# The joins between mixer, dense layer and routing: weight splits moved behind block 1's norm, a first product in halves, the router as one 16-column operand, a gather in four banks

## The reference, cut to what matters

```
for l in range(2):
    h = rms_norm(x, norm_mix[l])
    x = x + hybrid_mixer(h, w_in[l], conv_w[l], ..., w_out[l])     # conv, group norm, silu; gated unit
    h = rms_norm(x, norm_ffn[l])
    if l % 2 == 0:
        x = x + swiglu(h, ffn_wg[0], ffn_wu[0], ffn_wd[0])         # 1024 -> 2816 -> 1024
    else:
        logits = h @ router                                        # 1024 -> 8
        top_vals, top_idx = top_k(logits, 2); gates = softmax(top_vals)
        x = x + sum over e of gate[:, e] * swiglu(h, wg[e], wu[e], wd[e])
x = rms_norm(x, norm_final)
# then second_block: meta tokens, two attentions, gates, output product, norm
```

## Time and profile before

| | |
|---|---|
| median of 3 runs | 1587.92 us (1583.66 to 1600.85) |
| profiled execution, its own time | 1595.88 us |
| its span on the core | 1594.1 us |
| TensorE busy | 1521.7 us (95%) |
| VectorE busy | 1112.6 us (70%) |
| ScalarE busy | 902.7 us (57%) |
| mean granted TensorE clock | 0.966 of full speed |
| mean HBM traffic over the span | 263 GB/s |

### The profile page before, as it was taken

One profiled execution on the slowest core, in us unless ns is written; L12 is line 12 of the kernel. 1 busy time (PEld: TensorE's weight loads), 2 busy tenths in 40 slices (PEclk: granted clock), 3 DMA queues, 4 the chain that ended last, 5 costly groups with the idle time before them and its releaser, 6 DMA issues.

```text
span 1594.1 us, 19419 instructions
## 1 busy us (share of the span) xinstructions
PE 1521.7 (95%) x7672; PEld 1283.5 (81%) x7672; DVE 1112.6 (70%) x974; ACT 902.7 (57%) x765; POOL 98.6 (6%) x110
## 2 busy tenths in 40 slices
PE   6989999979889999999999999999999599999997
PEld 6869998878688888888888888888888496777785
DVE  6975555359668888888888888888788543333555
ACT  4554344235537677776777767676776353343452
POOL 3600000035010000000000000000100100000000
PEclk9999999989979999999999999999999797998999
DMA  9457974443429999999999999999998442232250
GB/s 303 146 168 238 323 250 172 132 138 129 146 76 404 357 379 378 364 391 355 386 366 366 394 348 404 350 387 370 368 400 308 149 159 79 80 104 81 80 185 27
DMA packets 118955, 408.21 MB, mean 256 GB/s; under 512 B 5840, under 2 KB 31616, under 8 KB 118896
## 3 DMA queue, kind: packets, MB, share of 16 engines
q1 hardware_dynamic: 114576, 392.84, 67.4%
q0 software_dynamic: 3104, 10.22, 1.8%
q10 hardware_dynamic: 1216, 4.33, 0.7%
HBM read 400.02 MB, written 19.40 MB: 263 GB/s over the span
## 4 chain that ended last, share of the span: by engine, by line
PE 86%; DVE 8%; ACT 2%; DMA 2%; issue 2%; ACTq 0%; SPq 0%; POOL 0%; DVEq 0%; POOLq 0%
PE ps L460 24%; PE ps L461 23%; PE ps L462 23%; DVE yT L1826 3%; DVE low L444 1%; PE ps L456 1%; PE ps L2433 1%; PE ps L2157 1%; PE ps L2121 1%; PE ps L2159 1%; PE ps L2158 1%; ACT high L433 1%; DMA raw<-in_moe_wu 1%; PE ps L1214 1%; PE ps L1235 1%
## 5 line engine op out<-in xcount | busy, mean ns | idle before, releaser
L450 DVE TENSOR_TENSOR low<-raw,high 128x2816 fp32r<-128x2816 f32 (+1 forms) x168 | 516.2, 3090 | 100.9 <-ACT high L439 100.8
L439 ACT ACTIVATE high<-raw 128x2816 fp32r<-128x2816 f32 (+1 forms) x168 | 428.4, 2560 | 104.3 <-PE ps L462 60.5
L460 PE MATMUL ps<-high,xTm_hi 128*128 128x512 f32 (+2 forms) x1152 | 428.0, 372 | 13.0 <-DVE xTm_lo L1863 6.2
L461 PE MATMUL ps<-low,xTm_hi 128*128 128x512 f32 (+2 forms) x1152 | 422.7, 367 | 0.0
L462 PE MATMUL ps<-high,xTm_lo 128*128 128x512 f32 (+2 forms) x1152 | 422.4, 367 | 0.0
L444 DVE TENSOR_TENSOR low<-raw,high 128x2816 fp32r<-128x2816 f32 (+2 forms) x72 | 203.1, 2827 | 81.0 <-ACT high L433 81.0
L460 PEld LDWEIGHTS ps<-high,xTm_hi 128*128 128x128 f32 x1152 | 217.8, 189 | 48.1 <-DVE xTm_lo L1863 6.7
L462 PEld LDWEIGHTS ps<-high,xTm_lo 128*128 128x128 f32 x1152 | 217.8, 189 | 28.4
L461 PEld LDWEIGHTS ps<-low,xTm_hi 128*128 128x128 f32 x1152 | 217.9, 189 | 28.0
L433 ACT ACTIVATE high<-raw 128x2816 fp32r<-128x2816 f32 (+2 forms) x72 | 168.4, 2343 | 113.4 <-PE ps L462 93.2
L460 PE MATMUL ps<-high,eT_hi 128*128 128x512 f32 x352 | 142.1, 404 | 0.0
(11 more groups left out here) (361 smaller groups left out, 1795.6 us busy)
## 6 DMA issues: line engine op xcount, KB each, us to landing
raw<-in_moe_wg SPq DMA_DIRECT2D x64, 1408.0 KB, 8.0
raw<-in_moe_wu SPq DMA_DIRECT2D x64, 1408.0 KB, 9.1
raw<-in_moe_wd SPq DMA_DIRECT2D x48, 1536.0 KB, 8.5
rawb<-in_w_in SPq DMA_DIRECT2D x25, 1024.0 KB, 5.1
raw<-in_w_in SPq DMA_DIRECT2D x16, 1024.0 KB, 5.7
raw<-in_moe_wd SPq DMA_DIRECT2D x16, 1024.0 KB, 8.5
raw<-in_ffn_wg SPq DMA_DIRECT2D x8, 1408.0 KB, 11.9
raw<-in_ffn_wu SPq DMA_DIRECT2D x8, 1408.0 KB, 11.1
```

The costliest lines, as they stand in the source:

```text
L439: nc.scalar.activation(high[:, j % SPLITS, 0:n], raw[:, j % RAWS, 0:n], ACT.Copy).then_inc(hi_made, 1)
L450: nc.vector.tensor_tensor(low[:, j % SPLITS, 0:n], raw[:, j % RAWS, 0:n], f(high[:, j % SPLITS, 0:n]), ALU.subtract).then_inc(lo_made, 1)
L460: nc.tensor.matmul(out, xh, wh, start=first, stop=False)
L461: nc.tensor.matmul(out, xh, wl, start=False, stop=False)
```

## The change

Eight edits, all at the three joins, at the mixers' tails and in the routing.

1. In `mixer`, VectorE does `group_scale(1)` ahead of the split of the next stage's first chunk, not behind it.
2. Join 1: 10 warm transposes for 30. The first product of block 0 is cut in two halves of four k tiles, and block 1's transposes stand between the halves.
3. Join 2: no warm transposes ahead; block 0's transposes come first, then 24 warm ones, then block 1's. The low part of the second chunk moves behind `xt_low` of block 1 on VectorE; its high part on ScalarE moves to stand between block 1's root and `xt_high`.
4. Join 3: 10 warm transposes for 30, and 8 more ahead of block 1's transposes. The low part of chunk `MOE0 + 1` leaves the join and is made behind the gather's reads, with chunk `MOE0 + 2`, ahead of the destination rows. In its place stand the high and low parts of the tokens themselves (`token_high`, `token_low`), which came after the join.
5. The router's high and low parts lie side by side, so the high part of the tokens is multiplied by both in one matmul of 16 columns: two matmuls per k tile for three. VectorE adds the two halves of the sums.
6. The comparisons of both blocks are done in one instruction each.
7. Between the five small products and the gather stand 8 warm transposes for 36.
8. The gather's four parts have a bank each, so none waits for a read, and chunk j of item 0 (j below 4) waits for part j alone.

The diff, cut to its core:

```
-                norm_std(n, 1)
-                xt_high(tn, 1)
+                norm_std(n, 1)
+                if between is not None:
+                    between()
+                xt_high(n, 1)
...
-            norm(2, 2)
+            norm(2, lambda: high_upto(LAYER_CHUNKS + 1))
...
-            norm(3, 3)
-            for b in range(NB):
-                nc.scalar.activation(xn_hi[:, b, :], xn[:, b, :], ACT.Copy).then_inc(xs_hi, 1)
+            norm(3, lambda: token_high(0))
+            token_high(1)
...
                 xt_low(n + 1, 0)
                 norm_apply(n + 1, xn, 1)
-                low_upto((MIX_CHUNKS, LAYER_CHUNKS, MOE0)[n] + 1)
+                if n == 0:
+                    low_upto(MIX_CHUNKS + 1)
+                elif n == 2:
+                    token_low(0)
                 xt_low(n + 1, 1)
+                if n == 1:
+                    low_upto(LAYER_CHUNKS + 1)
+                elif n == 2:
+                    token_low(1)
...
                 group_rstd(1)
+                group_scale(1)
                 low_upto(c0 + MIX_CHUNKS)
-                group_scale(1)
                 conv_low(1)
...
-            step(nc.vector.tensor_copy(logit[:, :, :], ps[:, 0, 0:NB * NE].rearrange("p (b e) -> p b e", b=NB)))
+            sums = ps[:, 0, 0:2 * NB * NE].rearrange("p (b h e) -> p b h e", b=NB, h=2)
+            step(nc.vector.tensor_copy(logit[:, :, :], sums[:, :, 0, :]))
+            step(nc.vector.tensor_tensor(logit[:, :, :], logit[:, :, :], sums[:, :, 1, :], ALU.add))
...
-                                      ps[:, TP[p % 2], 2 * P:4 * P].rearrange("p (t n) -> p t n", t=2)).then_inc(g0_freed, 1)
+                                      ps[:, GATHER_BANKS[p], 2 * P:4 * P].rearrange("p (t n) -> p t n", t=2)).then_inc(g0_freed, 1)
+            low_upto(MOE0 + 2)
...
-                if l:
-                    keep_warm(3, 30)
                 for b in range(NB):
                     norm_transposes(2 * l, 2 * l, b)
+                    if l and b == 0:
+                        keep_warm(3, 24)
...
-                    mm = first_products(1, product)
+                    keep_warm(3, 10)
+                    norm_transposes(1, 1, 0)
+                    pe.wait_ge(xt_lo, 4 + 2)
+                    pe.wait_ge(x_made, 4)
+                    product(0, range(4))
+                    norm_transposes(1, 1, 1)
+                    product(0, range(4, KT))
+                    pe.wait_ge(xt_lo, 4 + 4)
+                    mm = product(1)
...
-                    mm = three(ps[:, 0, b * NE:b * NE + NE], xT_hi[...], xT_lo[...], router_hi[:, k, :], router_lo[:, k, :], ...)
+                    nc.tensor.matmul(ps[:, 0, base:base + 2 * NE], xT_hi[...], router_both[:, k, :], ...)
+                    mm = nc.tensor.matmul(ps[:, 0, base:base + NE], xT_lo[...], router_hi[:, k, :], ...)
...
-            first_products(3, router_product).then_inc(logits_ready, 1)
+            keep_warm(3, 10)
+            norm_transposes(3, 3, 0)
+            pe.wait_ge(xt_lo, 12 + 2)
+            pe.wait_ge(x_made, 12)
+            router_product(0)
+            keep_warm(3, 8)
+            norm_transposes(3, 3, 1)
+            pe.wait_ge(xt_lo, 12 + 4)
+            router_product(1).then_inc(logits_ready, 1)
             keep_warm(3, 24)
...
-            keep_warm(3, 36)
+            keep_warm(3, 8)
...
-                if p >= 2:
-                    pe.wait_ge(g0_freed, p - 1)
...
-                        if first:
-                            pe.wait_ge(g0_freed, 4)
+                    if first and j < 4:
+                        pe.wait_ge(g0_freed, j + 1)
```

More of the change, by code:

```diff
@@ L356, in model_program @@
     HC = CC // 2
+    GATHER_BANKS = (4, 5, 6, 7)
     OUT_ROWS = (4, 6, 0, 2)
@@ L1532, in xt_high, with norm @@
                                          ps[:, banks[2 * b + m], :].rearrange("p (t n) -> p t n", t=4), ACT.Copy).then_inc(xt_hi, 1)
-            def norm(n, tn):
+            def norm(n, between=None):
                 norm_std(n, 0)
-                xt_high(tn, 0)
+                xt_high(n, 0)
                 norm_std(n, 1)
-                xt_high(tn, 1)
+                if between is not None:
+                    between()
+                xt_high(n, 1)
             def mixer(l):
@@ L1990, in _ @@
                                     ALU.subtract).then_inc(logit_made, 1)
[L1991 to L1998, removed]
+            pairs = [P, NB, NE, NE]
+            other = logit.rearrange("p b (o e) -> p b o e", o=1).to_broadcast(pairs)
+            own = logit.rearrange("p b (e o) -> p b e o", o=1).to_broadcast(pairs)
+            nc.vector.tensor_tensor(above[:, :, :, :], other, own, ALU.is_gt)
+            step(nc.vector.tensor_tensor(equal[:, :, :, :], other, own, ALU.is_equal))
+            step(nc.vector.tensor_tensor(equal[:, :, :, :], equal[:, :, :, :],
+                                         earlier.rearrange("p (o a) b -> p o a b", o=1).to_broadcast(pairs), ALU.mult))
+            step(nc.vector.tensor_tensor(above[:, :, :, :], above[:, :, :, :], equal[:, :, :, :], ALU.add))
+            step(nc.vector.tensor_reduce(rank[:, :, :], above[:, :, :, :], AX.X, ALU.add))
             nc.vector.tensor_scalar(chosen[:, :, :], rank[:, :, :], 1.5, None, ALU.is_lt).then_inc(chosen_made, 1)
@@ L2122, in norm_transposes @@
                     mm.then_inc(xt_filled, 1)
-            def first_products(n, product):
-                if n:
-                    keep_warm(3, 30)
[L2128 to L2134, removed]
             def token_transposes(src, banks, count):
@@ L2306, in _, with product @@
                 wh, wl = (slot_view(r, c % SPLITS, KT, TW) for r in (high, low))
-                def product(b):
+                def product(b, tiles=range(KT)):
                     pe.wait_ge(lo_made, c + 1)
-                    for k in range(KT):
+                    for k in tiles:
                         mm = three(ps[:, 2 * up + b, 0:TW], xT_hi[:, k, b * P:b * P + P], xT_lo[:, k, b * P:b * P + P],
@@ L2351, in router_product @@
             def router_product(b):
+                base = 2 * NE * b
                 for k in range(KT):
-                    mm = three(ps[:, 0, b * NE:b * NE + NE], xT_hi[:, k, b * P:b * P + P], xT_lo[:, k, b * P:b * P + P],
-                               router_hi[:, k, :], router_lo[:, k, :], k == 0, k == KT - 1)
-                return mm
-            first_products(3, router_product).then_inc(logits_ready, 1)
+                    nc.tensor.matmul(ps[:, 0, base:base + 2 * NE], xT_hi[:, k, b * P:b * P + P], router_both[:, k, :],
+                                     start=(k == 0), stop=False, skip_group_check=True)
+                    mm = nc.tensor.matmul(ps[:, 0, base:base + NE], xT_lo[:, k, b * P:b * P + P], router_hi[:, k, :],
+                                          start=False, stop=(k == KT - 1), skip_group_check=True)
+                return mm
+            keep_warm(3, 10)
[7 more added lines that the diff above has]
+            router_product(1).then_inc(logits_ready, 1)
             keep_warm(3, 24)
@@ L2375, in gather @@
                         for b in range(NB):
-                            mm = nc.tensor.matmul(ps[:, TP[p % 2], base + kk * P:base + kk * P + P],
+                            mm = nc.tensor.matmul(ps[:, GATHER_BANKS[p], base + kk * P:base + kk * P + P],
                                                   part[:, b, k * P:k * P + P], pick[:, b, :], start=(b == 0), stop=(b == 1))
@@ L2392, in item @@
                     pe.wait_ge(lo_made, chunk(i, j) + 1)
-                    if j == 0:
-                        if first:
-                            pe.wait_ge(g0_freed, 4)
-                        else:
-                            pe.wait_ge(tp_freed, fill_no(i, 0))
+                    if first and j < 4:
+                        pe.wait_ge(g0_freed, j + 1)
+                    if j == 0 and not first:
+                        pe.wait_ge(tp_freed, fill_no(i, 0))
                     if j == 4 and not first:
```

18 lines of the change are left out of this document (10 added, 8 removed).

## The result

| | before | changed |
|---|---|---|
| median of 6 runs each | 1588.79 us (1583.66 to 1600.85) | 1571.93 us (1565.85 to 1574.51) |
| profiled execution, its own time | 1595.88 us | 1572.29 us |
| its span | 1594.1 us | 1570.5 us |
| mean granted clock | 0.966 | 0.975 |

The ratio of changed to before is put at 0.986, with a 95% interval of 0.9821 to 0.9898: faster by 1 to 1.8%. The quotient of the two medians is 0.989 and lies at the upper end of that interval.

The account below looks back on a forecast made before the run. TensorE's pace was taken to bound the expert loop and dense layer, with gains left at the joins; 5.4 + 9.4 + 6.5 = 21.3 us off a median of 1587.9 gave 1567 us, range 1557 to 1577.

Parts of the forecast that it names:

- tail of mixer 0 and join 1: From mixer 0's last chunk to block 1's first dense product, which starts 5.4 us earlier.
- join 2 with the start of mixer 1: Dense output to mixer 1: start 8.7 us earlier, another 1.6 if the clock is up; half taken, 9.4 us.
- tail of mixer 1, join 3, routing: From mixer 1's last chunk to the gather, which starts 9.5 us earlier at the low clock, 15.4 at the high.
- item 0: First item of the expert loop: TensorE waits 4.5 us at chunk 3 for VectorE's low part; 4.2 us given back.
- 21.3 as weighted: Total gain in us: 5.4 + 9.4 + 6.5, the last part taken between 5.3 and 11.2.
- Tail (3.6 and 5.0): Scaling ahead of the split gains 3.6 us in mixer 0, 5.0 in mixer 1; 2.2 each if the clock falls.
- Join 1 (5.4 with the tail): Block 1's first dense product starts at 127.15 for 132.55; cutting the product in halves gives only 0.3 us of it.
- The open half, the clock: At mixer 1's start, 1.6 us more come if the clock is up; half was taken.
- the chance of a high clock: Rival: the clock holds in join 3, or the late low part costs less; gain 25 to 28 us; chance 0.17.
- the clock fell in join 3 and in neither tail: Rival: the clock falls at all joins and tails despite the fillers; gain 12 to 15 us; chance 0.13.
- the rival of absorption: The expert loop absorbs the early start because DMA sets its end; 1575 to 1590 us; chance 0.10.
- a load stream that falls behind: Expert loop loads enter one chunk behind and never catch up; loop 57 us longer, 1620 to 1625 us; chance 0.03.

Follow-up runs that it names:

- a1: The changed kernel itself, unchanged, compared again with the kernel before; median 1574.45 us, ratio 0.9895 (0.9859 to 0.9932).
- b1: The kernel before, unchanged, profiled once more; one execution, 1598.39 us.
- b2: The kernel before, unchanged, profiled another time; one execution, 1591.06 us.
- x1: The kernel before with the order of scaling and split turned in both mixers and nothing else; ratio 0.994 (0.9913 to 0.9967).
- x7: The changed kernel with block 0's first dense product in one piece ahead of block 1's transposes; run once, 1571.92 us.
- x4: The changed kernel with the low parts of chunks MOE0 + 1 and MOE0 + 2 made ahead of the gather's reads; median 1565.11 us, ratio to kernel before 0.9796.
- x6: The changed kernel with the router's high part again in two matmuls of 8 columns, without the extra addition; run once, 1576.35 us.
- x9: The changed kernel with old warm transpose counts: 30 for 10 in joins 1 and 3, 36 for 8 ahead of the gather; median 1570.95 us, ratio 0.9871.
- x3: The changed kernel with only chunk MOE0 + 1's low part moved from behind the gather into VectorE's idle stretch in join 3; median 1571.48 us, ratio 0.9823.
- x5: The changed kernel without the joins' warm transposes (10 in join 1, 24 in join 2, 10 and 8 in join 3); median 1576.17 us, ratio 0.9892.

## Why the prediction was right

The terms of the sum, read off the profiled executions (us; the last row is the time by which chunk 4 of item 0 starts earlier than 484.89):

| term | forecast | changed | a1 |
|---|---|---|---|
| tail of mixer 0 and join 1 | 5.4 | 5.6 | 5.2 |
| join 2 with the start of mixer 1 | 9.4 | 10.5 | 10.5 |
| tail of mixer 1, join 3, routing | 9.5 | 10.6 | 9.6 |
| item 0 | -4.2 | -3.3 | -3.4 |
| together | 20.1 (21.3 as weighted) | 23.4 | 21.9 |

**Tail (3.6 and 5.0).** Start of `out_chunk(3)` forecast 2.2 us earlier: measured 2.4 (110.58 for 113.06, of which 0.1 arose before the tail). The clock stayed up in all profiles with the edit. The 1.4 us for mixer 0's low clock were real in one profile of the kernel before and not in b1 and b2; against these two, chunk 4 starts 21.3 us earlier, not 23.4 (the rest of the difference is that their mixer 0 began 0.6 to 0.7 us earlier). The forecast read this price from one execution; that the same execution is the base of the table is luck. x1 shows the edit alone.

**Join 1 (5.4 with the tail).** 126.94 for the 127.15 forecast. The two sizes inside it hold too: the transposes wait 0.54 us for `xn`, and the halves are worth 0.32 us (x7).

**Join 2 (9.4).** 7.3 us to the first matmul, as forecast: 8.7 of the 10.5. The open half, the clock, came out up in the changed kernel and in a1, down for part of the first chunk in x4, x6, x7 and x9: taking the middle was fair. (The middle of 8.7 and 10.3 is 9.5, not 9.4.)

**Join 3 and routing (9.5).** From the first router product to the end of the second I had 11.0 us at the low clock and 7.2 at the high one; it took 10.1 and, in a1, 11.4. The clock fell within the first product, behind 2 matmuls of 16 in the changed kernel and behind 6 in a1, and was up again for the second in the changed kernel, low in a1. 16 columns cost as 8 (x6). The gather is held by `pick` alone, with a bracket of 0.43 us. Two parts of this term weren't undone by themselves: the comparisons in one instruction each, priced at nothing (the 0.6 us that they were to save are 0.45 by the forecast's own figures: ten of 0.23, less five of 0.33 and one of 0.2), and the banks of the gather, for which the trace has 3.60 us from the gather's start to item 0, where it had 5.11.

**Item 0 gives back 4.2: measured 3.3.** The mechanism held at each step. Chunk 3 was to start 19.8 us behind the gather and did so 19.7 behind it (436.35 to 456.05), against 18.0 before; the wait was to be 4.5 and was 4.08 and 4.13; the low clock followed. (Three chunks of 3.83 us behind a gather of 3.6 end at 15.1 us, not at the forecast's 15.4; measured are 15.6.) Its price was put too high, 2.3 us: chunk 3 took 5.47 us for 3.82, so it was 1.65. x4 takes the stall away, and from the gather to chunk 4 it is 6.2 us shorter. The forecast had named VectorE's order alone; x3 shows that with one low part moved ahead, VectorE waits 2.0 us for ScalarE's high part of chunk `MOE0 + 2`.

**Sum.** 21.3 us forecast, from 9.5 - 4.2 = 5.3 for the last part, raised to 6.5 for the chance of a high clock. Between the profiled executions it is 23.6, between milestones 21.4 to 23.3. Between medians it is 16.9 and, in a1's comparison, 16.4; by the ratio of 0.986 it would be 22; the intervals of the ratios (0.982 to 0.990 and 0.986 to 0.993) both hold 0.9866, which is what 21.3 us would be. Whether the medians are 5 us short by chance or not stays open. What is shown is that executions of the same kernel differ by 7 us behind the milestone, so the last few us of agreement between forecast and median, either way, say nothing of the mechanism.

**The rivals.** In the changed kernel the clock fell in join 3 and in neither tail, and even x5, where it fell at all three joins, kept it in the tails. The expert loop took nothing: from chunk 4 of item 0 (484.89 before, 461.52 now) to the milestone it is 758.8 us, and before 758.7; in all fourteen profiles it lies between 757.4 and 759.4. So neither the rival of absorption nor that of a load stream that falls behind came in. The price of the second was reckoned with a slip. The trace gives a chunk as 1408.0 KB, and its rows are 128 by 2816 numbers of four bytes, which is 1.442 MB and not 1.408: in 3.83 us that is 376 GB/s, not 368. The 377 GB/s of the earlier trace rows are thus about what TensorE's pace asks for, and show no room above it.

## What to carry to other kernels

Ask of each warm transpose whether the data behind it is already there. If it is, the transpose is a wait (1.2 to 1.4 us for 20 more in x9). If not, it fills time that was idle anyway, and the router's first product met a better clock the more of them stood ahead; in the other two joins they weren't enough each time. Where a split is moved behind a join to shorten it, write down the queue of every engine at its new place with the time at which each item is needed: that gave the new stall of 4 us before anything ran, and forgetting one engine (ScalarE in x3) made the first repair shorten the stall by 0.5 us and not 3, and bring chunk 4 no earlier. For gains of a few microseconds in a run of 1600, compare a milestone just behind the changed part, since whole runs differ by more further on, and take several profiles: the milestone too moved by 1.7 us between three profiles of the kernel before.

## What was not expected of the hardware

A stretch of 3.1 us in which TensorE is idle doesn't always bring the clock down: mixer 0's tail had 0.50 in one profile of the kernel before and 1.00 in two others with the same idle, and in nine profiles with the same join 2 the first chunk of mixer 1 started five times at 1.00 and four times at 0.50. The start of a run shifts everything behind it by up to 1.5 us (the variance product of mixer 0 at 100.1 to 101.6 in the profiles); whether this decides which level the clock has is not shown. A price of a low clock read from one profile is therefore that of one draw.
